# GpSimd in place of VectorE for one low part per pair in the RWKV-7 branch

## The chip, the cores and the metric

The kernel runs on one core of a Trainium2 chip. The metric is the time of the device for one launch, in microseconds (us). One execution was also taken with the hardware profiler; its trace gives start and duration of the instructions of every engine: TensorE (PE in the rows, PEld for its weight loads), VectorE (DVE), ScalarE (ACT), GpSimd (POOL) and SyncE (SP), which issues most of the loads.

## The reference, cut to what matters

A one-layer decoder trunk: RMSNorm, one combined input projection, two recurrent branches (HGRN2 and RWKV-7), a gated merge with an output projection, and a mixture of experts. The change touches the RWKV-7 branch alone and alters no value.

```python
z = xn @ w_in[l]                                  # xn: 512 x 2048
zq, zf, zi, zo, zs, zga, zgb = jnp.split(z, IN_SPLITS, axis=-1)
# RWKV-7, per head of 64 channels, one step per token:
sa = jnp.einsum('bhvk,bhk->bhv', state, at)
state = state * exp(lw) + sa * b + v * k
y = jnp.einsum('bhvk,bhk->bhv', state, rt)
# then: mean and variance over the head, rsqrt, scale, + bonus * v, * g
```

## The kernel before

The projection `xn @ w_in` is made in fp32 precision out of three fp32r products. Each weight block of 2048 x 128 (a "unit") is loaded by SyncE into a raw tile of 128 x 2048 (`in_raw`). ScalarE rounds it to a high part (`ring_hi`, L187, tile `in_hi`), and VectorE subtracts to get the low part (`ring_lo`, L192, tile `in_lo`). TensorE then runs 48 matmuls of 128x512 per unit (`dense_pass`, L160): high x high, high x low and low x high over 16 row blocks. There are two slots of each tile, so the units go round a ring. Three counters order it: `hi_done`, `lo_done` and `unit_done`. SyncE loads a unit into a slot once `lo_done` says that the unit two before has its low part, since the raw tile is free then.

The RWKV phase treats 16 heads as eight pairs, p = 0 to 7. In the first seven TensorE runs five units per pair, woven as filler (`dense(n)`) between the small matmuls of the recurrence, which works on eight chunks of 64 tokens. Each engine has one fixed list of work per pair, and a semaphore wait holds up all that stands behind it on that engine.

Where a pair ends, the lists are these.

- TensorE: six state matmuls (L1375), each behind the state that VectorE made before it, with three filler matmuls in between. Then 28 small matmuls (L1382, `y_done`), two for the bonus sum (L1386 and L1387, `bonus_sum`), 16 filler matmuls, then a wait for `sum_lo` and two matmuls for the variance (L1390 and L1391, `var_done`), and the remaining filler. The next pair begins with L1255.
- ScalarE: when unit 3 of the pair has been used (`unit_done`), it rounds the sixth unit, number 5, which is the first unit of the next pair (L187). After it come the sigmoid of a gate (L918), the squares of y (L991) and their high part (L994, `sum_hi`), and after the variance a logarithm (L996) and an exponential (L998).
- VectorE: six state updates (L1159), then the low part of unit 5 (`split(5)`, through L192), then bonus times v (L1164, waits for `bonus_sum`), the low part of the squares (L1167, waits for `sum_hi`, signals `sum_lo`), the normalisation (L1170 to L1174), and the output (L1177). The next pair begins with copies (L1046) and token shifts (L1055). Its own `split(1)` comes after L1077.
- GpSimd: stores the gate of unit 3 (L852), waits for the output, splits it into high and low (a cast at L355, a subtraction at L357), stores it (L359) and stores the other gate (L852).

The helper that moves from one engine to the other is this:

```python
def ring_lo(dve, ring, slot, m):
    dve.wait_ge(ring["hi_done"], m + 1)
    dve.tensor_tensor(ring["lo"][slot][:], ring["raw"][slot][:], ring["hi"][slot][:].bitcast(F32),
                      ALU.subtract).then_inc(ring["lo_done"], 1)
```

Of the kernel before, what the change touches and what calls it, by code (L numbers as in the profile page):

```python
# [140 lines left out]
def wait_apart(eng, passed, sem, value):  # L141


    eng.wait_ge(sem, value)
    eng.sem_inc(passed, 1)
# [44 lines left out]
# [4 lines that stand above are left out]
# [159 lines left out]
def store_split(pool, io, y, row, split, count, stored):  # L353

    pool.tensor_copy(y[:, 1, :], y[:, 0, :].bitcast(F32)).then_inc(split, 1)  # L355
    wait_apart(pool, io["pool_waits"], split, count + 1)
    pool.tensor_tensor(y[:, 0, :], y[:, 0, :].bitcast(F32), y[:, 1, :].bitcast(F32), ALU.subtract).then_inc(split, 1)  # L357
    wait_apart(pool, io["pool_waits"], split, count + 2)
    pool.dma_start(io["y_split"][bass.ds(row, 1)].rearrange("a p c t -> p (a c) t"), y[:].bitcast(F32)).then_inc(stored, 16)  # L359
# [357 lines left out]
def phase_rwkv(nc, io, keep, block, sems, early):  # L717
# [9 lines left out]
    FIRST = 3 + 3  # L727
    UNITS = 3 + HG_GATES
    LAST_UNITS = 2 * HG_GATES
    BASE = (HEADS - 1) * (4 + HG_GATES) + 4  # L730
# [6 lines left out]
    with ExitStack() as ctx:  # L737
        mem = Memory(nc, ctx)
        ring, z, z_read = keep["ring"], keep["z"], keep["z_read"]
# [66 lines left out]
        def gate_rows(p, last):  # L806

            own = [HG_GATES * (HEADS + p) + g for g in range(HG_GATES)]
            return own + [HG_GATES * (HEADS - 1) + g for g in range(HG_GATES)] if last else own

        @block.sync
        def _(sp):
            for u in range(3):
                ring_load(sp, ring, u % 2, BASE + u, w_in[:, :, (LORA_COL, LORA_COL + P, LORA_COL + 288 - P)[u]:][:, :, 0:P])

            def lora(p, col):
                wait_apart(sp, ring["passed"], lora_done, 3 * p + 3)
                up = lambda w: w[:, bass.ds(col, P)]
                sp.dma_start(w_wa[0:HALF, :], up(io["rw_w_up"][0])).then_inc(lora_in, 16)
                sp.dma_start(w_wa[HALF:P, :], up(io["rw_a_up"][0])).then_inc(lora_in, 16)  # L820
                sp.dma_start(w_g1[:], up(io["rw_g_up"][0][0:P, :])).then_inc(lora_in, 16)
                sp.dma_start(w_g2[96:P, :], up(io["rw_g_up"][0][P:, :])).then_inc(lora_in, 16)

            def pair_units(p, q, last):

                cols = [] if last else [RW_COL + WIDTH * u + P * (p + 1) for u in range(3)]
                cols += [GATE_COL + P * row for row in gate_rows(p, last)]
                for u, col in enumerate(cols):
                    ring_load(sp, ring, (q + u) % 2, BASE + FIRST + UNITS * p + u, w_in[:, :, bass.ds(col, P)])

            for u in range(3):
                ring_load(sp, ring, (3 + u) % 2, BASE + 3 + u, w_in[:, :, RW_COL + WIDTH * u:RW_COL + WIDTH * u + P])
            with sp.Fori(0, PAIRS // 2 - 1) as j:
                for q in range(2):
                    lora(2 * j + q, P * (2 * j + q))
                    pair_units(2 * j + q, q, False)
            for q in range(2):
                lora(PAIRS - 2 + q, P * (PAIRS - 2 + q))
                pair_units(PAIRS - 2 + q, q, q == 1)

        @block.gpsimd
        def _(pool):
            pool.sem_inc(y_free, 1)
            pool.sem_inc(gate_free, 1)

            def store(p, q, half, last):
                def store_gate(g):

                    u = g if last else 3 + g
                    wait_apart(pool, keep["pool_waits"], z_read[(q + u) % 2],  # L850
                               TURN + UNITS * half + (FIRST + UNITS * q + u) // 2 + 2)
                    pool.dma_start(io["gate"][bass.ds(gate_rows(p, last)[g], 1)].rearrange("a p t -> p (a t)"),  # L852
                                   gates[g][:]).then_inc(gate_stored, 16)

                for g in range(LAST_UNITS if last else 1):
                    store_gate(g)
                if last:
                    return
                wait_apart(pool, keep["pool_waits"], y_ready, p + 1)
                store_split(pool, io, y_out, HEADS + p, y_split, 2 * p, y_stored)  # L860
                store_gate(1)
                pool.wait_ge(y_stored, 16 * p + 16)
                pool.sem_inc(y_free, 1)
                pool.wait_ge(gate_stored, 16 * HG_GATES * (p + 1))
                pool.sem_inc(gate_free, 1)

            with pool.Fori(0, PAIRS // 2 - 1) as j:
                for q in range(2):
                    store(2 * j + q, q, j, False)
            for q in range(2):  # L870
                store(PAIRS - 2 + q, q, PAIRS // 2 - 1, q == 1)
# [138 lines left out]
        def _(dve):  # L1010
# [29 lines left out]
            def pair(p, q, half, last):  # L1040
                order = Order(dve, dve_o, DVE_STEPS * p)
                tt = dve.tensor_tensor
                split = lambda u: ring_lo(dve, ring, (q + u) % 2, BASE + FIRST + UNITS * p + u)
# [8 lines left out]
                for u in (1, 2):  # L1052
# [23 lines left out]
                cum_c = chunked(cum)  # L1076
                tt(chunked(dl), cum_c[:, :, RW_CHUNK - 1:RW_CHUNK].to_broadcast([P, N_CHUNKS, RW_CHUNK]), cum_c,  # L1077
                   ALU.subtract).then_inc(decays_ready, 1)
                split(1)

                dve.wait_ge(w_a_ready, 2 * p + 2)
# [74 lines left out]
                for c in range(1, N_CHUNKS - 1):  # L1156
# [1 line left out]
                    dve.wait_ge(s_ready, (N_CHUNKS - 1) * p + c)  # L1158
                    dve.scalar_tensor_tensor(state[:, c + 1, :], state[:, c, :], g_last[:, c:c + 1],  # L1159
                                             twin[1][:, 1, HALF * c:HALF * c + HALF], ALU.mult, ALU.add).then_inc(s_ready, 1)  # L1160
                split(5)

                dve.wait_ge(bonus_sum, p + 1)
                tt(bonus[:], twin[1][:, 0, :], v[:], ALU.mult).then_inc(bonus_read, 1)  # L1164
# [32 lines left out]
            with dve.Fori(0, PAIRS // 2 - 1) as j:  # L1197
                for q in range(2):
                    pair(2 * j + q, q, j, False)
            for q in range(2):  # L1200
                pair(PAIRS - 2 + q, q, PAIRS // 2 - 1, q == 1)
# [1377 lines left out]
```

## Time and profile before

| | |
|---|---|
| time, median of three runs | 2668.78 us (2668.69 to 2672.29) |
| time of the profiled execution | 2672.34 us |
| its span, first to last instruction | 2670.7 us |
| TensorE matmul busy | 2517.0 us, 94% |
| VectorE busy | 1135.8 us, 43% |
| ScalarE busy | 815.6 us, 31% |
| GpSimd busy | 105.6 us, 4% |
| RWKV phase in the trace | about 586 to 1290 us |
| seven pairs of it | one every 80.1 us |

A row of a timeline gives the start in us from the beginning of the span, the duration in us, the engine, the line of the kernel, the operation, the tiles (output, arrow, inputs), their shapes, and in brackets the idle time of the engine before the instruction, with what ended it. A matmul's end is modelled: neighbouring 128x512 matmuls start 0.23 us apart although each is shown as 0.39 us long. A busy share of 94% is therefore not TensorE at its peak, but a gap in the starts is time lost.

### The profile page before, as it was taken

What the parts mean: (1) busy time and instruction counts of PE and PEld (TensorE: products, weight loads), DVE (VectorE), ACT (ScalarE), POOL (GpSimd) and SP (SyncE); (2) the same over time, 40 slices, a digit from 0 to 9 for tenths busy, and PEclk for the clock granted to TensorE, in tenths of its full rate; (3) what the DMA queues carried; (4) which work ended last, traced back from release to release, by engine and by line L of the source; (5) the groups of instructions that cost most, each with busy time, mean ns of one, the idle gap of its engine ahead of it and who ended that gap; (6) DMA issues with size and microseconds to landing.
All of it is one profiled execution on the core that took longest, in us unless ns stands there. A gap on an engine that the chain in (4) does not pass through costs nothing.

```text
span 2670.7 us, 40372 instructions
## 1 busy us (share of the span) xinstructions
PE 2517.0 (94%) x15789; PEld 1695.0 (63%) x15789; DVE 1135.8 (43%) x1648; ACT 815.6 (31%) x1010; POOL 105.6 (4%) x136
## 2 busy tenths in 40 slices
PE   7999999999999999999999998898999989998896
PEld 5888888877787777787788876333333333333342
DVE  5333433344666666666444233332333223323234
ACT  5333444443344445444322222021111111111112
POOL 0000000010000000000000000000000000000000
PEclk9999999999999999999999999899999999999998
DMA  5333333333223232223754534999999999999995
GB/s 169 95 110 110 97 100 93 110 99 93 83 68 88 78 95 80 83 69 92 246 147 141 170 104 187 397 421 421 422 421 422 421 422 422 422 421 422 422 421 218
DMA packets 312384, 594.43 MB, mean 223 GB/s; under 512 B 17098, under 2 KB 238918, under 8 KB 260550
## 3 DMA queue, kind: packets, MB, share of 16 engines
q1 hardware_dynamic: 303372, 559.71, 57.2%
q0 software_dynamic: 8912, 33.22, 3.2%
q8 instruction: 83, 1.36, 0.2%
q14 instruction: 17, 0.14, 0.0%
HBM read 578.02 MB, written 24.64 MB: 226 GB/s over the span
## 4 chain that ended last, share of the span: by engine, by line
PE 75%; DMA 17%; DVE 3%; issue 2%; ACT 1%; SPq 0%; DVEq 0%; ACTq 0%
PE in_z L160 36%; DMA ex_w_up<-in_expert_w_up_dram 17%; PE bank L2399 10%; PE bank L2426 4%; PE bank L2386 1%; PE in_z L150 1%; PE in_z L152 1%; PE mg_z_rw L152 1%; PE mg_z_rw L150 1%; PE in_z L151 1%; PE mg_z_rw L151 1%; DVE in_lo L192 1%; PE rw_b L1315 1%; PE bank L2387 1%; PE in_z L1603 1%
## 5 line engine op out<-in xcount | busy, mean ns | idle before, releaser
L160 PE MATMUL in_z<-xn_hi,in_hi 128*128 128x512 f32 x1440 | 569.4, 395 | 4.7 <-DVE in_lo L192 3.2
L160 PE MATMUL in_z<-xn_hi,in_lo 128*128 128x512 f32 x1440 | 571.7, 397 | 0.0
L160 PE MATMUL in_z<-xn_lo,in_hi 128*128 128x512 f32 x1440 | 564.2, 392 | 0.0
L2399 PE MATMUL bank<-ex_w_gate,ex_xt_sb 128*64 128x512 f32 x768 | 359.3, 617 | 55.9 <-DMA ex_w_up<-in_expert_w_up_dram 55.9
L192 DVE TENSOR_TENSOR in_lo<-in_raw,in_hi 128x2048 fp32r<-128x2048 f32 x122 | 281.6, 2308 | 284.0 <-ACT in_hi L187 167.7
L2401 PE MATMUL bank<-ex_w_up,ex_xt_sb 128*64 128x512 f32 x768 | 360.1, 618 | 0.0
L160 PEld LDWEIGHTS in_z<-xn_hi,in_hi 128*128 128x128 f32 x1440 | 271.1, 188 | 64.9 <-issue 5.3
L160 PEld LDWEIGHTS in_z<-xn_lo,in_hi 128*128 128x128 f32 x1440 | 270.8, 188 | 58.0 <-issue 1.9
L160 PEld LDWEIGHTS in_z<-xn_hi,in_lo 128*128 128x128 f32 x1440 | 271.0, 188 | 55.5
L2399 PEld LDWEIGHTS bank<-ex_w_gate,ex_xt_sb 128*64 128x64 f32 x768 | 104.9, 142 | 278.9 <-issue 278.8
L2426 PE MATMUL bank<-ex_w_down,const 128*64 128x512 f32 x512 | 227.8, 598 | 2.4 <-ACT const L2312 0.6
L2428 PE MATMUL bank<-ex_w_down,const 128*64 128x512 f32 x512 | 227.9, 598 | 0.0
L2165 DVE TENSOR_TENSOR h<-bank,h 128x512 f32<-128x512 f32 x240 | 149.0, 682 | 178.1 <-PE bank L2387 177.9
L187 ACT ACTIVATE in_hi<-in_raw 128x2048 fp32r<-128x2048 f32 x89 | 169.7, 1907 | 46.2 <-PE in_z L160 43.1
L2155 DVE SCALAR_TENSOR_TENSOR logits_t<-bank,rs_slot,logits_t 64x512 f32<-64x512 f32 x32 | 23.8, 744 | 345.2 <-ACT logits_t L2310 344.7
L2310 ACT ACTIVATE logits_t<-bank,rs_slot 64x512 f32<-64x512 f32 x32 | 21.9, 683 | 485.2 <-PE bank L2401 485.2
L2426 PEld LDWEIGHTS bank<-ex_w_down,const 128*64 128x64 f32 x512 | 67.9, 137 | 138.5 <-issue 138.4
L2320 ACT ACTIVATE ex_y_rows<-bank,ex_w_slot 64x512 f32<-64x512 f32 x128 | 87.4, 683 | 220.2 <-PE bank L2428 217.7
L1520 ACT ACTIVATE in_hi<-in_raw 128x2048 fp32r<-128x2048 f32 x30 | 57.5, 1918 | 234.4 <-PE mg_z_rw L152 122.5
L2401 PEld LDWEIGHTS bank<-ex_w_up,ex_xt_sb 128*64 128x64 f32 x768 | 104.9, 141 | 0.0
L2386 PE MATMUL bank<-ex_y_high,const_as_r 128*128 128x512 f32 x240 | 100.8, 420 | 0.0
L2191 DVE TENSOR_TENSOR ex_y_low<-ex_y_rows,ex_y_high 128x1024 fp32r<-128x1024 f32 x32 | 39.2, 1226 | 132.4 <-ACT ex_y_high L2324 132.4
(505 smaller groups left out, 3481.9 us busy)
## 6 DMA issues: line engine op xcount, KB each, us to landing
ex_w_down<-in_expert_w_down_dram SPq DMA_DIRECT2D x128, 1024.0 KB, 21.2
ex_w_gate<-in_expert_w_gate_dram SPq DMA_DIRECT2D x96, 1024.0 KB, 23.0
ex_w_up<-in_expert_w_up_dram SPq DMA_DIRECT2D x96, 1024.0 KB, 26.0
in_raw<-in_w_in_dram SPq DMA_DIRECT2D x91, 1024.0 KB, 5.7
in_raw<-in_w_out_dram SPq DMA_DIRECT2D x32, 512.0 KB, 4.7
ex_w_gate0b<-in_expert_w_gate_dram SPq DMA_DIRECT2D x16, 1024.0 KB
ex_w_up0b<-in_expert_w_up_dram SPq DMA_DIRECT2D x16, 1024.0 KB
rt_then_ex_w<-in_expert_w_gate_dram SPq DMA_DIRECT2D x16, 1024.0 KB
```

What stands on the lines that cost most here:

```text
L150: pe.matmul(out, w_hi, x_hi, start=first, stop=False, skip_group_check=True)
L160: return pe.matmul(out, w[:, k, :], x[:, k, :], start=(n == 0), stop=(n == PASSES * KT - 1), skip_group_check=True)
L187: act.activation(ring["hi"][slot][:], ring["raw"][slot][:], ACT.Copy).then_inc(ring["hi_done"], 1)
L192: dve.tensor_tensor(ring["lo"][slot][:], ring["raw"][slot][:], ring["hi"][slot][:].bitcast(F32), ALU.subtract).then_inc(ring["lo_done"], 1)
L1520: act.activation(ring["hi"][slot][:], ring["raw"][slot][:], ACT.Copy).then_inc(ring["hi_done"], 1)
L2165: dve.tensor_tensor(part, bank[SPREAD_BANKS[o]][:], part, ALU.add).then_inc(added, 1)
L2320: act.activation(y[halves[u], f:f + D_EXPERT], down_ps[c][part, :], ACT.Copy, scale=w_slot[part, :]).then_inc(y_read, 1)
L2386: pe.matmul(bank[b][:], rows, y_hi[:, f:f + D_EXPERT], start=True, stop=False, skip_group_check=True)
L2399: pe.matmul(gate_up[low, :], x_t[:, k, halves[u]], w_gate[n][u][:, j, :], start=start, stop=stop, skip_group_check=True)
L2401: mm = pe.matmul(gate_up[high, :], x_t[:, k, halves[u]], w_up[n][u][:, j, :], start=start, stop=stop, skip_group_check=True)
L2426: pe.matmul(down_ps[c][low, :], h_t[:, n, :], w_down[n][:, lo_c:lo_c + D_EXPERT], start=(n == 0), stop=(n == DC - 1), skip_group_check=True)
L2428: mm = pe.matmul(down_ps[c][high, :], h_t[:, n, :], w_down[n][:, hi_c:hi_c + D_EXPERT], start=(n == 0), stop=(n == DC - 1), skip_group_che ...
```

## The change

For the first seven pairs GpSimd makes the low part of unit 5. It is put ahead of the gate stores in GpSimd's list of the pair. VectorE does it only in the last pair. Since `lo_done` is one counter that both engines now raise, VectorE waits, before its `split(1)`, until the low part of unit 0 of the pair (the one that GpSimd made) has been counted.

```diff
@@ GpSimd, store(p, q, half, last)
+                if not last:
+                    ring_lo(pool, ring, (q + 5) % 2, BASE + FIRST + UNITS * p + 5)
                 for g in range(LAST_UNITS if last else 1):
                     store_gate(g)
@@ VectorE, pair(p, q, half, last)
                    ALU.subtract).then_inc(decays_ready, 1)
+                dve.wait_ge(ring["lo_done"], BASE + FIRST + UNITS * p + 3)
                 split(1)
@@ VectorE, behind the state updates
-                split(5)
+                if last:
+                    split(5)
```

## Rows read from the trace of the kernel before

**Rows 1.** The page's busy time by engine, and its chain of waits by engine.

```profile
PE 2517.0 (94%) x15789; PEld 1695.0 (63%) x15789; DVE 1135.8 (43%) x1648; ACT 815.6 (31%) x1010; POOL 105.6 (4%) x136
...
PE 75%; DMA 17%; DVE 3%; issue 2%; ACT 1%; SPq 0%; DVEq 0%; ACTq 0%
```

**Rows 2.** The seven pairs' stretch: busy us (count) by engine, granted clock, DMA share.

```profile
640.00:1260.00 620.00, 615.21 (x6738) 486.96 (x6737) 401.98 (x539) 278.10 (x351) 27.39 (x37) 1.00 0.30 82
```

**Rows 3.** TensorE's waits in that phase: line <- releaser: us total, times, longest.

```profile
PE in_z L160 <- DVE in_lo L192: 3.2, 9, 1.6
```

**Rows 4.** VectorE by time, first pair: start us, us, instruction [idle before].

```profile
715.25 0.28 DVE L1159 SCALAR_TENSOR_TENSOR rw_tm<-rw_tm,rw_g_last,rw_b 128x64 f32<-128x64 f32 x1 [0.63 <-PE rw_b L1375]
716.56 2.29 DVE L192 TENSOR_TENSOR in_lo<-in_raw,in_hi 128x2048 fp32r<-128x2048 f32 x1 [1.03 <-ACT in_hi L187]
718.77 0.68 DVE L1164 TENSOR_TENSOR rw_k<-rw_b,rw_v 128x512 f32<-128x512 f32 x1
720.30 0.69 DVE L1167 TENSOR_TENSOR rw_kb_r<-rw_sq,rw_kb_r 128x512 fp32r<-128x512 f32 x1 [0.85 <-ACT rw_kb_r L994]
...
728.35 0.91 DVE L1055 TENSOR_TENSOR rw_lw<-rw_zc 128x512 f32<-128x512 f32 x1 [0.21 <-DVE rw_one_ka L1048]
729.18 1.76 DVE L1055 TENSOR_TENSOR rw_cum<-rw_zc 128x512 f32<-128x512 f32 x1
...
738.32 0.69 DVE L1074 TENSOR_SCALAR rw_sq<-rw_b 128x512 f32<-128x512 f32 x1 [2.16 <-PE rw_b L1262]
...
740.12 2.28 DVE L192 TENSOR_TENSOR in_lo<-in_raw,in_hi 128x2048 fp32r<-128x2048 f32 x1
```

**Rows 5.** ScalarE in order of time, first pair.

```profile
714.62 1.91 ACT L187 ACTIVATE in_hi<-in_raw 128x2048 fp32r<-128x2048 f32 x1 [6.15 <-PE in_z L160]
716.55 1.28 ACT L918 ACT_TABLE_LOAD   x1
...
719.57 0.63 ACT L994 ACTIVATE rw_kb_r<-rw_sq 128x512 fp32r<-128x512 f32 x1
...
721.82 0.69 ACT L996 ACTIVATE rw_ba<-rw_b,rw_eps 128x512 f32<-128x512 f32 x1 [0.32 <-PE rw_b L1391]
```

**Rows 6.** TensorE in order of time, around two hand-overs from VectorE.

```profile
720.82 0.39 PE L160 MATMUL in_z<-xn_hi,in_lo 128*128 128x512 f32 x1
721.05 0.50 PE L1390 MATMUL rw_b<-rw_kb_r,rw_block_r 128*128 128x512 f32 x1
...
741.90 0.39 PE L160 MATMUL in_z<-xn_hi,in_lo 128*128 128x512 f32 x1
742.54 0.49 PE L160 MATMUL in_z<-xn_hi,in_hi 128*128 128x512 f32 x1 [0.25 <-DVE in_lo L192]
```

**Rows 7.** GpSimd in order of time, first pair.

```profile
719.24 0.55 POOL L852 DMA_DIRECT2D scratch_gate<-rw_e_neg  x1 [128.74 <-ACT rw_e_neg L918]
728.10 0.61 POOL L355 CAST rw_y_out<-rw_y_out 128x512 fp32r<-128x512 f32 x1 [8.31 <-DVE rw_y_out L1177]
728.90 1.50 POOL L357 TENSOR_TENSOR rw_y_out<-rw_y_out 128x512 fp32r<-128x512 f32 x1 [0.18 <-POOL rw_y_out L355]
```

**Rows 8.** The one 128x2048 GpSimd subtraction, in the norm phase.

```profile
20.75 4.54 POOL L316 TENSOR_TENSOR in_lo<-in_raw,in_hi 128x2048 fp32r<-128x2048 f32 x1 [20.18 <-ACT in_hi L268]
```

**Rows 9.** ScalarE ahead of it: the rounding that releases it.

```profile
18.76 1.91 ACT L268 ACTIVATE in_hi<-in_raw 128x2048 fp32r<-128x2048 f32 x1 [2.77 <-DMA in_raw<-in_w_in_dram]
```

**Rows 10.** VectorE beside it; two inputs from PSUM and SBUF.

```profile
21.50 5.36 DVE L308 SCALAR_TENSOR_TENSOR xn_lo<-x_tr,par,xn_hi 128x512 fp32r<-128x512 f32 x8 [3.03 <-ACT xn_hi L273]
```

**Rows 11.** Instructions of one line: xcount: ns min/median/max, first and last start.

```profile
L1167 DVE TENSOR_TENSOR rw_kb_r<-rw_sq,rw_kb_r x8: 691/693/694, 720.3 to 1287.0; 128x512 fp32r<-128x512 f32 x8
...
  PEld rw_b L1390: 1.9, 7
```

**Rows 12.** A GpSimd subtraction of the HGRN2 phase.

```profile
586.21 3.11 POOL L357 TENSOR_TENSOR hg_y<-hg_y 128x512 fp32r<-128x512 f32 x1 [0.18 <-POOL hg_y L355]
```

**Rows 13.** VectorE in the same microseconds.

```profile
585.64 2.53 DVE L192 TENSOR_TENSOR in_lo<-in_raw,in_hi 128x2048 fp32r<-128x2048 f32 x1 [0.40 <-ACT in_hi L187]
```

## The prediction, made before the result was known

> **What bounds the kernel now.** I read the page first: TensorE is busy for 94% of the span and carries 75% of the chain of waits, VectorE 3% [rows 1]. In the stretch that the change touches this is sharper: of 620 us TensorE's matmuls fill 615.21, VectorE's work 401.98 and GpSimd's 27.39, at a full clock [rows 2]. So a microsecond saved on VectorE is worth something only where TensorE waits for it. Of those waits, the one on low parts comes to 3.2 us in nine times [rows 3], and the timeline shows that the regular one is not the low part being moved but `split(1)` of the next pair: it ends at 740.12 + 2.28 = 742.40, and the matmul behind it starts at 742.54, 0.64 us after its neighbour where 0.23 is usual [rows 4, 6]. The low part of unit 5 is ready at 718.85 and first used by TensorE after 730, in the next pair. Nobody waits for it.
>
> What happens behind it decides. ScalarE ends the high part of unit 5 at 714.62 + 1.91 = 716.53, loads a table, makes a gate and the squares, and ends the squares' high part (L994) at 720.20 [rows 5]. VectorE has finished the low part by then, has done L1164, and sits idle for 0.85 us until ScalarE releases L1167, which runs from 720.30 to 720.99 [rows 4]. TensorE's L1390 needs it and starts at 721.05, just 0.23 us behind its neighbour of 720.82 [rows 6]: no time is lost, but none is spare either, for its weight load was held in seven pairs, 1.9 us in all [rows 11]. The pairs repeat this within hundredths; L1167 lasts 691 to 694 ns in all eight [rows 11].
>
> **The change part by part.** *Removed from VectorE:* seven subtractions of 2.29 us, 16.0 us [rows 4]. L1164 moves up by about 1 us, to the end of the bonus matmuls, and then VectorE waits longer for ScalarE: L1167 is released by L994, whose place in ScalarE's list does not change. Gain on the path: 0. Were ScalarE earlier, L1390 still could not start before its neighbours are done.
>
> *Added to GpSimd:* seven subtractions of the same tiles. The norm phase has one: 4.54 us, starting 0.08 us after the high part that releases it (20.67 to 20.75) [rows 8, 9]. The state chain is over at 715.53 [rows 4] when the high part is still being made, so this work cannot lie beside the chain. With 0.10 us to pick it up, GpSimd runs it from 716.63 to 721.17. TensorE wants the result nine microseconds later, so its length alone costs nothing. But it covers 720.30, where VectorE starts L1167, an operation with both inputs in SBUF (`rw_sq`, `rw_kb_r`).
>
> *What the two do to each other* stands in the same trace, one pair boundary on. GpSimd's subtraction of 128x512 (L357) starts at 728.90, while VectorE is in a shift of two SBUF inputs: that shift takes 0.91 us, where L1167 of the same size takes 0.69. The next shift starts at 729.18 and takes 1.76 us, to 730.94; GpSimd's ends at 730.40 [rows 4, 7]. A quarter of 4.54 us is 1.14 us, and the second shift lost 1.07 us: it stood still for as long as GpSimd's operation ran, and ended 0.54 us after it. In the HGRN2 phase the order is the other way: VectorE's low part started first and lost only 2.53 - 2.29 = 0.24 us, while GpSimd's subtraction took 3.11 us instead of 1.14 [rows 12, 13]. The one that comes second stands still. An operation with one input in PSUM is not touched: eight of L308 beside the 4.54 us operation take 5.36 us, 0.67 each [rows 8, 10]; L1164 is of that kind.
>
> In the changed kernel GpSimd is first. L1167 stands still until about 721.17 and ends 0.54 us later, at 721.71, which is 0.72 us later than 720.99. TensorE then has run out of work: the hand-over takes 0.14 us in the second case of [rows 6], against the 0.06 us that it takes at 721.05 now. So L1390 starts at 721.71 + 0.06 to 0.14, 0.72 to 0.80 us late. I take 0.80, as the stalled hand-over is the one that resembles it. Seven pairs: 5.6 us.
>
> Rows show a hold of about 1.1 us, not one of 4.5 us. If GpSimd gave the port away in the middle, L1167 would lose less. From below: nothing, or the 0.24 us that the first comer lost [rows 13], 1.7 us over seven pairs. From above: L1164 stands still too, ends at 721.71, and L1167 follows a pitch of 0.60 us behind, a delay of 1.40 us with the hand-over, 9.8 us in all. I take the full hold of L1167 alone, since all of the 1.1 us hold in the rows was exclusive.
>
> The Trainium skill, "SBUF — State Buffer", section "Who interferes with whom", says that a VectorE instruction with two SBUF inputs and a GpSimd instruction that reads SBUF exclude each other, that the first comer keeps the shared pair for its whole instruction, and that the other blocks fully. By this rule the hold lasts the whole 4.54 us, and the sum is the 5.6 us above; the trace agrees for the 1.1 us case. Against my 4.54 us speaks "Perfetto Trace Analysis", section "GPSIMD Engine Instruction", which calls the spans of GpSimd instructions in a profile unreliable. Should the reads be over early, the sum would be smaller; the 0.54 us between the two ends, read at VectorE, is the check that this trace allows.
>
> *What the stall moves.* L1391, L996, L998 and the normalisation follow L1390, all later by the same 0.80 us as TensorE's own filler. VectorE reaches the next pair that much later, but so does TensorE, and VectorE's L1074 waits 2.16 us for TensorE there anyhow [rows 4]. So the delay neither grows nor is won back, and everything behind the phase moves with it.
>
> *Moved on GpSimd:* the gate store of 719.24 [rows 7] stands behind the subtraction and goes out at about 721.2. Its tile is written again after 741; no cost. *Moved on SyncE:* the load that `lo_done` of unit 5 releases goes out near 721.2 instead of 718.9 and is for a high part that ScalarE makes after 744; no cost, and SyncE has only loads of later units behind it. If that cover were gone, at most the 2.3 us that the low part is later would be at stake.
>
> *Added wait on VectorE:* before `split(1)`, at 740.12, for a count reached at 721.2, 19 us before. Behind it stands the low part that TensorE does wait for, so what the instruction itself takes would be lost. VectorE's sequencer runs ahead of operations of 0.6 us pitch; I take 0, at most 0.1 us each, 0.7 us in all.
>
> **The sum.** Profiled execution: 2672.34 + 5.6 = 2677.9 us. It lies 3.56 us above the median of the runs shown; the same 5.6 us on the median 2668.78 gives 2674.4 us.
>
> **The rivals.**
> - *GpSimd does not stop L1167, or lets it in early.* It decides from the point where GpSimd holds its reads for less than 720.30 - 716.63 = 3.67 us, or hands the port over between pieces. Then the change costs 0 to 1.7 us: 2668.8 to 2670.5, no change. For it: rows show only holds of 128x512. Against it: the second shift got nothing for its whole wait [rows 4, 7].
> - *The hold is wider*, L1164 included: 9.8 us, 2678.6 us. Against it: L308 ran at its pace beside GpSimd [rows 10].
> - *Faster.* VectorE is 2.29 us lighter per pair, and the regular wait before 742.54 goes away. That would give back 0.64 - 0.23 = 0.41 us in seven pairs, 2.9 us: 2665.9. Against it: VectorE waits for TensorE at L1074 in between [rows 4], so what it gains earlier does not reach `split(1)`.
> - That GpSimd's work is beside the state chain, as the change says, I hold to be wrong by 1.1 us, 715.53 against 716.63; it is part of every case.
>
> **How the numbers follow.** The forecast (5 to 7 us slower) has 0.61, the first rival 0.22, the wider hold 0.11, the faster one 0.06. A measurement of this kernel tells about 0.2%, 5.3 us, from no change, and the forecast lies almost on that line: a little over half of its chance, 0.38, is beyond it. Slower by over 0.2%: 0.38 + 0.11 = 0.49. Faster by over 0.2%: 0.03, half of that rival's chance, since its own price stays below the line. Within: 0.23 + 0.22 + 0.03 = 0.48. Though the two are as good as even, the time is that of the forecast. The range runs from just below the first rival, 2667.8, to just above the wider hold, 2679.3; the forecast's own is 2673.3 to 2676.0.
>
> **What would show it.** Right: in the seven pairs GpSimd's `in_lo` starts about 0.1 us after L187 ends and lasts 4.5 us; L1167 lasts about 1.4 us instead of 0.69 and ends some 0.54 us after it; L1390 starts 0.8 us late with idle time in front of it that names L1167; L1164 keeps 0.68 us; the pairs come every 80.9 us instead of every 80.1. Wrong: L1167 keeps 0.69 us (first rival), L1164 is stretched (wider hold), or the idle time before the matmul that follows `split(1)` shrinks (faster).

## The result, and the profile after

The changed kernel takes 2677.88 us (median of nine, 2677.43 to 2680.34), the kernel before 2672.29 us in the nine runs beside it (2668.69 to 2675.65). The ratio is 1.0024, with a 95% interval from 1.0015 to 1.0033: slower by 0.24%, which is 6.4 us (interval 4.0 to 8.8 us); between the two medians lie 5.6 us. The profiled span grew from 2670.7 to 2676.1 us.

The page's row of busy times, after, against [rows 1]:

```profile
PE 2516.7 (94%) x15789; PEld 1693.7 (63%) x15789; DVE 1125.5 (42%) x1641; ACT 815.5 (30%) x1010; POOL 137.3 (5%) x143
```

VectorE lost 10.3 us of busy time and GpSimd gained 31.7, seven operations of 4.6 us. VectorE gave up seven times 2.29 = 16.0 us, so 5.7 us came back; 7 x 0.78 = 5.5 of them are time in which it stood still, as the next rows show. VectorE in the first pair, after (start us, us, instruction, idle time before it), against [rows 4]; the lines of the kernel have moved by up to four:

```profile
715.24 0.28 DVE L1162 SCALAR_TENSOR_TENSOR rw_tm<-rw_tm,rw_g_last,rw_b 128x64 f32<-128x64 f32 x1 [0.64 <-PE rw_b L1379]
717.61 0.69 DVE L1168 TENSOR_TENSOR rw_k<-rw_b,rw_v 128x512 f32<-128x512 f32 x1 [2.09 <-PE rw_b L1391]
720.28 1.47 DVE L1171 TENSOR_TENSOR rw_kb_r<-rw_sq,rw_kb_r 128x512 fp32r<-128x512 f32 x1 [1.98 <-ACT rw_kb_r L996]
...
739.08 0.69 DVE L1076 TENSOR_SCALAR rw_sq<-rw_b 128x512 f32<-128x512 f32 x1 [2.16 <-PE rw_b L1266]
...
740.89 2.28 DVE L192 TENSOR_TENSOR in_lo<-in_raw,in_hi 128x2048 fp32r<-128x2048 f32 x1
```

ScalarE and GpSimd there, against [rows 5, 7]:

```profile
714.60 1.91 ACT L187 ACTIVATE in_hi<-in_raw 128x2048 fp32r<-128x2048 f32 x1 [6.16 <-PE in_z L160]
...
719.55 0.63 ACT L996 ACTIVATE rw_kb_r<-rw_sq 128x512 fp32r<-128x512 f32 x1
...
722.58 0.69 ACT L998 ACTIVATE rw_ba<-rw_b,rw_eps 128x512 f32<-128x512 f32 x1 [1.10 <-PE rw_b L1395]
```

```profile
716.60 4.60 POOL L192 TENSOR_TENSOR in_lo<-in_raw,in_hi 128x2048 fp32r<-128x2048 f32 x1 [126.17 <-ACT in_hi L187]
721.16 0.56 POOL L852 DMA_DIRECT2D scratch_gate<-rw_e_neg  x1
```

ScalarE ends the high part at 716.51. GpSimd starts at 716.60, 1.1 us after the last state update has ended, and works until 721.20. The bonus multiplication (now L1168, one input in PSUM) moves up to 717.61 and keeps 0.69 us. The split of the squares (now L1171, both inputs in SBUF) starts at 720.28 as before, released by ScalarE, and takes 1.47 us instead of 0.69: it ends at 721.75, 0.55 us after GpSimd.

TensorE, after, against [rows 6]; the last two rows are the end of the second pair and the start of the third, which is a turn of the loop over pairs:

```profile
720.82 0.39 PE L160 MATMUL in_z<-xn_hi,in_lo 128*128 128x512 f32 x1
721.81 0.50 PE L1394 MATMUL rw_b<-rw_kb_r,rw_block_r 128*128 128x512 f32 x1 [0.60 <-DVE rw_kb_r L1171]
...
743.30 0.49 PE L160 MATMUL in_z<-xn_hi,in_hi 128*128 128x512 f32 x1 [0.25 <-DVE in_lo L192]
...
809.10 0.39 PE L160 MATMUL in_z<-xn_hi,in_lo 128*128 128x512 f32 x1
810.68 0.66 PE L1259 MATMUL rw_b<-rw_low,rw_w_wa 64*128 64x512 f32 x1 [1.20 <-issue]
```

L1394 (before: L1390) starts 0.99 us behind its neighbour where 0.23 was enough: 0.76 us. The wait for `split(1)` is what it was, 0.25 us. Then there is something that the prediction does not have. At the turn TensorE stands for 1.20 us in front of L1259, with nothing in the profile that it waited for. The same place before:

```profile
807.57 0.39 PE L160 MATMUL in_z<-xn_hi,in_lo 128*128 128x512 f32 x1
808.08 0.66 PE L1255 MATMUL rw_b<-rw_low,rw_w_wa 64*128 64x512 f32 x1
```

TensorE's waits from 620 to 1290 us, after (total, times, longest), against [rows 3]:

```profile
PE rw_b L1394 <- DVE rw_kb_r L1171: 4.3, 7, 0.7
PE in_z L160 <- DVE in_lo L192: 3.2, 9, 1.5
...
PE rw_b L1259 <- issue: 2.3, 2, 1.2
```

So there are two new groups of idle time: seven times 0.60 us in front of the variance matmuls, and 2.3 us at the two turns of the loop (1.20 and 1.07), where before had 0 and 0.23.

The start of the first pair to the start of the eighth is the measure that the experiments below use, since it holds all that was touched: 1208.42 - 647.91 = 560.51 us before, 1215.77 - 647.87 = 567.90 us after, 7.39 us more. In the shares of the seven pairs this is 0.80, 1.84, 0.76, 1.61, 0.89, 0.76 and 0.73 us; the two large ones are the pairs that end at a turn. What follows the eighth start took 1462.3 us before and 1460.3 after, and in the other traces of this study that leave it alone from 1459.3 to 1465.0 us, without order. This scatter of the rest (its cause was not looked for) is why a difference of 2 us is seen in the stretch and not in the median.

### The profile page after: what moved, and what is told of

The parts are those of the page before. It is cut to its first block, busy times and chain, and to the rows that moved or that the text cites. A ratio compares the mean times of both kernels' runs of the same rounds, so it can differ in the third digit from the quotient of the medians.

```text
span 2676.1 us, 40374 instructions
## 1 busy us (share of the span) xinstructions
PE 2516.7 (94%) x15789; PEld 1693.7 (63%) x15789; DVE 1125.5 (42%) x1641; ACT 815.5 (30%) x1010; POOL 137.3 (5%) x143
## 4 chain that ended last, share of the span: by engine, by line
PE 74%; DMA 16%; DVE 4%; ACT 2%; issue 2%; SPq 0%; DVEq 0%; ACTq 0%
PE in_z L160 35%; DMA ex_w_up<-in_expert_w_up_dram 16%; PE bank L2403 11%; PE bank L2430 4%; PE bank L2390 1%; PE in_z L150 1%; PE in_z L151 1%; PE mg_z_rw L151 1%; PE mg_z_rw L150 1%; PE in_z L152 1%; PE mg_z_rw L152 1%; DVE in_lo L192 1%; PE rw_b L1319 1%; PE bank L2391 1%; ACT in_hi L187 1%
## 5 line engine op out<-in xcount | busy, mean ns | idle before, releaser
L192 DVE TENSOR_TENSOR in_lo<-in_raw,in_hi 128x2048 fp32r<-128x2048 f32 x115 | 265.5, 2309 | 276.7 <-ACT in_hi L187 160.4
```

## The experiments

Twelve further runs were made, eleven of them of other kernels. "Stretch" is the time from the first to the eighth pair's first matmul in each one's trace. Times are compared with the kernel before on the same chip.

| kernel | stretch, us | idle at the two turns, us | squares' split, us | ratio to before (95%) |
|---|---|---|---|---|
| before | 560.51 | 0, 0.23 | 0.69 | |
| changed | 567.90 | 1.20, 1.07 | 1.47 | 1.0024 (1.0015 to 1.0033) |
| e12_after_again (the changed kernel) | 568.03 | 1.27, 0.99 | 1.46 | one run, 2677.97 us |
| e1_wait_only | 560.86 | 0.29, 0.27 | 0.69 | 0.9999 (0.9990 to 1.0008) |
| e3_half | 561.34 | 0.29, 0.52 | 0.69 | 0.9997 (0.9988 to 1.0006) |
| e9_twelve | 562.74 | 1.03, 0.89 | 0.69 | one run, 2673.72 us |
| e10_fourteen | 563.98 | 1.09, 1.05 | 0.91 | one run, 2675.75 us |
| e2_psum_operand | 565.60 | 1.85, 1.85 | 0.69 | 1.0028 (1.0017 to 1.0038) |
| e7_memsets | 566.44 | 2.37, 2.26 | 0.69 | 1.0025 (1.0016 to 1.0034) |
| e4_behind | 566.90 | 0, 0, then 2.3 and 2.5 behind them | 0.69 | 1.0024 (1.0015 to 1.0033) |
| e5_dve_late | 562.93 | 1.24, 1.61 | 0.69 | 1.0007 (0.9998 to 1.0016) |
| e6_small_load | 566.10 | 0, 0 | 1.46 | 1.0026 (1.0017 to 1.0035) |
| e8_split1_early | 556.73 | 0.28, 0 | 0.69 | 0.9986 (0.9977 to 0.9995) |
| e11_both_early | 556.86 | 0, 0 | 0.69 | 0.9976 (0.9966 to 0.9986) |

### The wait alone

```diff
+                dve.wait_ge(ring["lo_done"], BASE + FIRST + UNITS * p + 3)
                 split(1)
```

> The kernel before with the new wait on VectorE alone; VectorE still makes the low part of unit 5. Theory (GpSimd's subtraction keeps VectorE's two-SBUF-input operation L1167 standing): the wait costs nothing, 0 to 0.7 us on the kernel before, and the matmul behind split(1) keeps its 0.17 to 0.25 us of idle time. Rival (the wait, or the count that it reads, makes the difference): 5 to 6 us slower, with the loss in front of the matmul behind split(1).

Measured: 2671.24 against 2671.01 us. TensorE's waits for the low parts are the old ones, those of [rows 3]:

```profile
PE in_z L160 <- DVE in_lo L192: 3.2, 9, 1.6
```

The new wait costs nothing that can be seen. The count that it waits for had been reached long before.

### How much of the tile GpSimd reads

The code is written shorter here than in the kernels.

```diff
-                    ring_lo(pool, ring, (q + 5) % 2, BASE + FIRST + UNITS * p + 5)
+                    pool.wait_ge(ring["hi_done"], BASE + FIRST + UNITS * p + 6)
+                    pool.tensor_tensor(lo[:, 0:K, :], raw[:, 0:K, :], hi[:, 0:K, :], ALU.subtract)   # K = 8, 12, 14 of 16
```

> The changed kernel, but GpSimd subtracts only 1024 of the 2048 columns (half of the low part of unit 5 is left out). Theory: GpSimd's operation lasts 2.3 us, from 716.6 to 718.9, is over before 720.3, so VectorE's split of the squares keeps 0.69 us, and the time is that of the kernel before, within 1 us; freeing VectorE of the work gains nothing. A rival in which GpSimd's being used at all, or the new order of the counts, costs the time expects 5 us slower still; a rival in which the lighter VectorE is worth something expects 1 to 3 us faster than before.

> The changed kernel, with GpSimd subtracting 1536 of the 2048 columns (the last quarter of the low part is left out). Theory: its operation lasts 3.45 us, 716.6 to 720.05, just short of the 720.28 at which VectorE's split of the squares starts: that keeps 0.69 us and TensorE does not wait in the pairs. The released load is 1.1 us earlier than in the changed kernel, so the idle time at the two turns lies between before's 0 to 0.3 us and the 1.85 us of the kernel with the PSUM operand. Rival (the hold goes on after the operation has ended, or depends on something else than overlap): 0.8 us or more.

> The changed kernel, with GpSimd subtracting 1792 of the 2048 columns (the last eighth is left out). Theory: its operation ends at 720.6 and VectorE's split of the squares, started at 720.28, stands still until then: it ends 0.54 us after it, at 721.2, and so lasts 0.9 us instead of 0.69 (0.69 at 1536 columns, 1.47 at 2048); TensorE's idle time in front of the variance matmul is about 0.1 us. Rival (the hold is of one length once it catches VectorE): 1.4 us or more as with 2048 columns.

Measured: with 1024 columns the time is that of before, 2671.01 us for both, and the stretch is 0.8 us longer, 0.6 of it at the two turns. VectorE's split of the squares keeps its length:

```profile
719.90 0.69 DVE L1174 TENSOR_TENSOR rw_kb_r<-rw_sq,rw_kb_r 128x512 fp32r<-128x512 f32 x1 [1.98 <-ACT rw_kb_r L999]
```

It keeps it with 1536 columns too, where GpSimd takes 3.50 us instead of the 3.45 expected and still ends short of the split. With 1792 columns GpSimd's end and the split overlap, first pair (GpSimd, then VectorE):

```profile
716.98 4.04 POOL L858 TENSOR_TENSOR in_lo<-in_raw,in_hi 128x1792 fp32r<-128x1792 f32 x1 [126.19 <-ACT in_hi L187]
```

```profile
720.66 0.91 DVE L1174 TENSOR_TENSOR rw_kb_r<-rw_sq,rw_kb_r 128x512 fp32r<-128x512 f32 x1 [1.99 <-ACT rw_kb_r L999]
```

GpSimd ends at 721.02 and the split 0.55 us later, at 721.57. TensorE's variance matmul then starts 0.44 us behind its neighbour instead of 0.23, a loss of 0.2 us where about 0.1 was expected. So the split takes 0.69, 0.69, 0.91 and 1.47 us at 1024, 1536, 1792 and 2048 columns: where the two overlap, it ends 0.55 to 0.56 us after GpSimd's operation, in all seven pairs of both kernels. The point from which the "not slower" rival decides, 3.67 us, lies between 3.50 (no hold) and 4.04 (held). The half kernel also shows that a VectorE lighter by 2.29 us in seven pairs gains nothing here. With 1536 and 1792 columns the turns cost 0.9 to 1.1 us each, which is most of what the first of these two kernels loses in the stretch and half of what the second does.

### One input from PSUM, and a GpSimd that only writes

```diff
-                tt(sum_parts[1], sq[:], sum_parts[0].bitcast(F32), ALU.subtract).then_inc(sum_lo, 1)
+                tt(sum_parts[1], twin[1][:, 0, :], sum_parts[0].bitcast(F32), ALU.max).then_inc(sum_lo, 1)
```

> The changed kernel, but VectorE's split of the squares takes its first input from PSUM (the bonus sum, of the same shape) in place of SBUF, with a maximum for the subtraction: the variance is not the reference's. Theory: an operation with one SBUF input does not meet GpSimd, so it keeps 0.69 us beside GpSimd's 4.6 us, and the seven stalls are gone: 5.3 us less than the changed kernel, less what the turns of the loop cost. On the turns: if the later load is their cause, their idle time stays and grows by up to 0.76 us each (2 to 4 us slower than before in all); if TensorE's stall is the cause, none and the time of before. Rival to the theory (any VectorE operation is held while GpSimd reads): the operation lasts 1.47 us and the time is that of the changed kernel, 5 to 6 us above before.

GpSimd and VectorE, first pair:

```profile
715.64 4.59 POOL L192 TENSOR_TENSOR in_lo<-in_raw,in_hi 128x2048 fp32r<-128x2048 f32 x1 [125.50 <-ACT in_hi L187]
```

```profile
719.33 0.69 DVE L1171 TENSOR_TENSOR rw_kb_r<-rw_b,rw_kb_r 128x512 fp32r<-128x512 f32 x1 [1.99 <-ACT rw_kb_r L996]
```

The operation lies inside GpSimd's 4.59 us and keeps 0.69: with one SBUF input it is not held. (It is also a maximum in place of a subtraction; L1168 of the changed kernel, a multiplication with one input in PSUM, is not held either.) The second kernel keeps VectorE's instruction and changes GpSimd's (shortened; `lo5` is the tile of the low part):

```diff
-                    ring_lo(pool, ring, (q + 5) % 2, BASE + FIRST + UNITS * p + 5)
+                    wait_apart(pool, keep["pool_waits"], ring["hi_done"], BASE + FIRST + UNITS * p + 6)
+                    pool.memset(lo5[:, 0:8, :], 0.0)     # and, each behind the one before it,
+                    pool.memset(lo5, 0.0)
+                    pool.memset(lo5, 0.0).then_inc(ring["lo_done"], 1)
```

> The changed kernel, but GpSimd fills the low part with zeros by three memsets (0.9 and twice 1.8 us with 0.2 us between, about 716.6 to 721.5) instead of subtracting: it is as busy across 720.3, and reads nothing from SBUF; the low part of the unit is left out. Theory (it is GpSimd's reading that VectorE's second SBUF input meets): VectorE's split of the squares keeps 0.69 us, no idle time in front of the variance matmuls; with the later load at the turns 2 to 5 us slower than before. Rival (any GpSimd operation on SBUF holds VectorE): the split of the squares lasts until the memset running at 720.3 ends, 1.2 us or more longer, in seven pairs.

```profile
717.02 1.81 POOL L862 MEMSET in_lo<- 128x2048 f32 x1 [0.15 <-POOL in_lo L860]
```

```profile
717.57 0.69 DVE L1177 TENSOR_TENSOR rw_kb_r<-rw_sq,rw_kb_r 128x512 fp32r<-128x512 f32 x1 [1.99 <-ACT rw_kb_r L1002]
```

The split starts 0.55 us into a memset of 1.81 us and ends before it, unheld. In these runs both halves of the condition are needed: two SBUF inputs on VectorE, and a GpSimd operation that reads SBUF.

Yet neither kernel was fast. Their stretches are 5.1 and 5.9 us longer than before, with idle time at the turns of 1.85 us and more. The turns can carry a loss of this size by themselves. In these two kernels and in e4_behind another 1.6 to 1.7 us are lost in the pair that follows the second turn. The trace shows where: TensorE's granted clock falls there to 0.50 for 3.41 us, the lower of its two levels (1.2 instead of 2.4 GHz), which costs half of that time. In the kernel with the PSUM operand, in the columns of [rows 2], just behind the second turn and after it:

```profile
971.70:975.10 3.40, 3.40 (x7) 1.51 (x5) 3.33 (x6) 1.20 (x2) 1.10 (x2) 0.50 0.55 220
975.20:978.60 3.40, 3.40 (x16) 2.70 (x15) 1.91 (x2) 3.02 (x4) 0.00 (x0) 1.00 0.02 6
```

Before it fell, TensorE had stood for 1.85 us up to 970.79. The same idle time at the first turn of this kernel was not followed by a fall. In the other eleven traces the clock is not lowered anywhere in the stretch.

### GpSimd behind the split of the squares

```diff
+                    pool.wait_ge(sum_lo, 3 * p + 3)
                     ring_lo(pool, ring, (q + 5) % 2, BASE + FIRST + UNITS * p + 5)
```

> The changed kernel, with GpSimd waiting for the split of the squares on VectorE (sum_lo) before its subtraction, which then runs from about 721.1 to 725.7; TensorE wants it at about 730. Theory, first part: VectorE's split of the squares keeps 0.69 us and the seven stalls of 0.76 us in front of the variance matmuls are gone. Second part (the trace of the changed kernel shows 1.20 and 1.07 us of idle time of TensorE at the two turns of the loop over pairs, where the trace of before shows 0 and 0.23; the 1 MB load that lo_done of unit 5 releases then runs 3 us closer to the turn): the load here goes out at 725.9, so it runs right across the turn, and the idle time there is 1.2 us or more, twice: 2 to 5 us slower than before in all. Rival to the second part (the idle time at the turn comes from TensorE's own stall in the pair): none at the turn, and the time is that of before, within 1 us.

Measured: 2676.6 us, 1.0024, as slow as the changed kernel, with no hold in any pair. The first part holds. The second holds in kind, with more than the 1.2 us each that it asked for, though the idle time has moved to the filler matmuls behind the turn:

```profile
PE in_z L160 <- issue: 4.8, 2, 2.5
```

The stretch is 6.4 us longer than before and the median 5.6 us higher, more than the 2 to 5 us expected. The 6.4 us are 4.8 us of this idle time, and 1.7 us of the lowered clock.

### The late low part without GpSimd

```diff
-                split(5)
-
                 dve.wait_ge(bonus_sum, p + 1)
...
                 tt(sum_parts[1], sq[:], sum_parts[0].bitcast(F32), ALU.subtract).then_inc(sum_lo, 1)
+                split(5)
```

> The kernel before, with no work moved to GpSimd: VectorE makes the low part of unit 5 behind its split of the squares instead of ahead of it (about 721.0 to 723.3). No engine shares anything new, TensorE's matmuls in front of the variance are not held, and only lo_done of unit 5 and with it the 1 MB load of the unit two behind come 4.4 us later. Theory (the load that runs into the turn of the loop over pairs holds up what TensorE needs to go on there): idle time of TensorE of 1.5 to 2.5 us at or just behind each of the two turns, 3 to 6 us slower than before, as with the two kernels in which GpSimd did the work without a stall in the pair. Rival (GpSimd's subtraction or its stores cause the idle time at the turn): none beyond the 0.2 to 0.3 us of before, and its time within 1 us.

Measured: idle times of 1.24 and 1.61 us at the turns, the stretch 2.42 us longer, in a kernel in which GpSimd does nothing new:

```profile
PE rw_b L1254 <- issue: 2.9, 2, 1.6
```

That is less than the 3 to 6 us expected, and the total (2673.14 against 2670.95, an interval that includes 1) cannot tell it from nothing. The idle time itself is clear, and GpSimd is not its cause.

### The load cut to a sixteenth

The edit is shortened here.

```diff
+                    if q == 0 and u == 2:
+                        wait_apart(sp, ring["passed"], ring["lo_done"], BASE + FIRST + UNITS * p + u + 1)
+                        sp.dma_start(ring["raw"][u % 2][:, 0:1, :], w_in[:, 0:1, bass.ds(col, P)]).then_inc(...)
+                        continue
```

> The changed kernel, but in every other pair the load that lo_done of unit 5 releases (the third of SyncE's five) brings 64 KB in place of 1 MB; the rest of that weight block keeps old values. Those are the loads ahead of the two turns of the loop. Theory: the seven stalls of L1394 stay (0.60 us of idle time each, 5.3 us in all), but the 1.20 and 1.07 us at the turns fall to 0.3 or less, so the time is 2 us below the changed kernel. Rival (the idle time at the turn is a consequence of TensorE's own stall, or of GpSimd): both stay and the time is that of the changed kernel.

All waits of TensorE in the stretch and the last pair:

```profile
PE rw_b L1398 <- DVE rw_kb_r L1175: 4.3, 7, 0.7
PE in_z L160 <- DVE in_lo L192: 3.2, 9, 1.5
PE in_z L1431 <- issue: 2.5, 1, 2.5
PE rw_b L1329 <- issue: 0.9, 1, 0.9
PE rw_b L1323 <- DVE rw_step L1134: 0.6, 1, 0.6
```

The row of the turn is gone, the seven holds of 0.60 us stand as they were, and the stretch falls by 1.80 us to 566.10. The total did not follow: 2678.59 against 2677.88 us, where 2 us less was expected. The intervals of the two ratios (1.0017 to 1.0035 and 1.0015 to 1.0033) overlap almost wholly, so the totals cannot tell 2 us; what this run shows rests on the stretch. Left over are 5.59 us more than before in the stretch, about the size of the prediction's sum; the seven holds of 0.76 us are 5.3 of them.

The two rows of SyncE show what had moved, the load that the low part of unit 5 releases in the second pair, before and after:

```profile
799.12 0.37 SPq L181 DMA_DIRECT2D in_raw<-in_w_in_dram  x1
```

```profile
802.23 0.37 SPq L181 DMA_DIRECT2D in_raw<-in_w_in_dram  x1
```

It goes out 3.1 us later, 0.76 of it TensorE's own shift, and still 7.3 us before the turn is due; before it was 9.0. By this distance, from the load's issue to the matmul's start without its idle time: 9.0, 8.8 and 8.7 us (before, e1, e3) go with 0 to 0.3 us of idle time at the first turn (0.5 at e3's second); 7.6, 7.3 and 7.3 (e9, e10, changed) with 1.0, 1.1 and 1.2; 6.5 and 6.1 (e2, e7) with 1.9 and 2.4; 4.5 (e5) with 1.2 (1.6 at the second); and at 1.8 (e4) the turn is passed and 2.3 us are lost behind it.

Distance alone gives no rule, but the DMA records of the traces do. They hold packets of 16 KB of the kind `instruction` (queue 8), and one of them starts just ahead of every turn. The profile's DMA view of 0.1 us around its start, before (804.80 to 804.90) and after (807.60 to 807.70):

```profile
q8 instruction: 1, 0.02, 85.1%
```

```profile
q8 instruction: 1, 0.02, 74.9%
```

| kernel, first turn | last filler matmul | load's packets | fetch starts | first matmul behind the turn | from fetch to it | idle, us |
|---|---|---|---|---|---|---|
| e6_small_load | 808.90 | 803.1 to 804.1 | 806.18 | 809.40 | 3.22 | 0 |
| before | 807.57 | 800.1 to 805.2 | 804.84 | 808.08 | 3.24 | 0 |
| changed | 809.10 | 803.6 to 807.6 | 807.62 | 810.68 | 3.06 | 1.20 |
| e5_dve_late | 807.73 | 804.7 to 809.9 | 806.46 | 809.36 | 2.90 | 1.24 |
| e2_psum_operand | 806.61 | 802.0 to 806.2 | 805.76 | 808.85 | 3.09 | 1.85 |
| e7_memsets | 804.80 | 800.8 to 804.6 | 804.49 | 807.56 | 3.07 | 2.37 |

In all 28 turns of the 14 traces the first matmul comes 2.8 to 3.2 us after the start of this fetch. What differs is where the fetch stands against TensorE's own work: 2.7 us ahead of the last filler matmul in e6, 1.5 us in the changed kernel, 0.3 us in e7, and the idle time is longer by nearly what the fetch is later (to within 0.3 us). In e4 the load's packets run from 806.3 to 811.8, so this fetch is in time (3.05 us ahead, no idle time), and the next one is late instead: it starts 2.92 us behind the first matmul of the turn where before it was 0.25, and the filler matmul that stood for 2.3 us follows it by 2.45. So TensorE waits for instructions, and they are fetched late when the load's packets are under way. The queue does not carry the name of an engine; that it is TensorE's follows from these intervals. By what the load holds the fetch back is not shown.

### A trace of the changed kernel once more

> The changed kernel once more, unchanged, for its trace. Theory (late load into the turn): again 1 us or more of idle time of TensorE at each of the two turns of the loop over pairs. Rival (chance of one execution): 0.3 us or less.

Measured: 1.27 and 0.99 us at the turns, and the holds in all seven pairs. Both traces have the idle time at both turns, so it is part of the change's cost and not the chance of one execution.

### Where VectorE does have a gap that helps

```diff
                    ALU.subtract).then_inc(decays_ready, 1)
-                split(1)
...
+                split(1)
                 dve.wait_ge(kk_sum, p + 1)
```

> The kernel before, with VectorE's low part of unit 1 (split(1)) moved ahead of its wait for the sum of kk, into the 2.16 us in which it waits for TensorE. Its high part is ready 6 us earlier. Theory: the matmul that follows it no longer waits (0.17 to 0.25 us of idle time, 0.41 us between starts lost in each of eight pairs), the operations behind L1074 are 0.1 us later at most: 2.5 to 3.5 us less than before, about 0.1%. Rival: the load that lo_done of unit 1 releases then runs 3 us earlier and the chain of kk starts later, and TensorE waits for the operands instead: no gain or a loss of up to 1 us.

Measured: 2667.15 us, ratio 0.9986 (0.9977 to 0.9995); the stretch is 3.78 us shorter. VectorE, first pair, and what is left of TensorE's waits for low parts, once in the last pair:

```profile
735.45 2.29 DVE L192 TENSOR_TENSOR in_lo<-in_raw,in_hi 128x2048 fp32r<-128x2048 f32 x1
737.77 0.69 DVE L1075 TENSOR_SCALAR rw_sq<-rw_b 128x512 f32<-128x512 f32 x1
```

```profile
PE in_z L160 <- DVE in_lo L192: 1.5, 1, 1.5
```

A pair takes 79.5 us where it took 80.0, a little more than the 0.41 us counted. For the last wait, rounding and low part of unit 2 in the last pair go where the other pairs have them:

```diff
                 if not last:
                     read_out(0)
-                    split(2)
+                split(2)
                 act.wait_ge(tok_done, 3 * p + 1)
...
-                if not last:
-                    split(2)
+                split(2)
                 dve.wait_ge(tok_done, 3 * p + 3)
...
-                if last:
-                    split(2)
```

> The kernel with split(1) early, and in the last pair the rounding and the low part of unit 2 put where the other pairs have them, ahead of the copies of the token-major tiles. Theory: TensorE's one wait of 1.5 to 1.6 us for a low part in the last pair is gone as well: 1.5 us less than the kernel with split(1) early, 4.5 to 5 us (0.18%) less than before. Rival: ScalarE's copies in the last pair start 1.9 us later and TensorE waits for them instead: no further gain.

Measured: 2663.62 us against 2671.04, ratio 0.9976 (0.9966 to 0.9986). No wait for a low part is left among TensorE's waits from 620 to 1290 us, of which these are all:

```profile
PE in_z L1419 <- issue: 2.4, 1, 2.4
PE rw_b L1311 <- DVE rw_step L1123: 0.6, 1, 0.6
```

The first matmul of the merge (L1419) starts 69.44 us after the start of the last pair, in the kernel with split(1) early 71.16: 1.7 us, where 1.5 was expected. This version beats both kernels, the one before by 0.24%. Its interval overlaps that of the kernel with split(1) early alone, so the last step rests on the trace.

## Why the prediction was right, and where it was not

*The total.* Right. Forecast 5.6 us slower, 2674.4 us on the median shown and 2677.9 on the profiled execution; measured 5.6 us between the medians and 6.4 us by the ratio. That the medians agree to the tenth is luck: the interval of the ratio goes from 4.0 to 8.8 us, and the stretch alone shows 7.4. The kernel before had a median of 2672.29 us over nine runs where the three shown first gave 2668.78; that is why the absolute time agrees with the upper of the two figures and lies above the forecast's own bounds, 2673.3 to 2676.0. (These bounds are 4.5 and 7.2 us above 2668.78, a little wider than the "5 to 7 us" of its words.)

*VectorE's lighter list gains nothing:* right. L1171 still starts at 720.28, and with half the columns the time is that of before.

*GpSimd's work:* 4.60 us against 4.54, picked up in 0.09 us against 0.10, and beside nothing of the state chain: right.

*The hold:* right in kind and size. L1171 ends at 721.75 where 721.71 was worked out, L1394 is 0.76 us late where 0.72 to 0.80 was, and the full hold behind a long operation, which no row of before showed, is shown by the series of columns. The Trainium skill, "SBUF — State Buffer", section "Who interferes with whom", says that a VectorE instruction with two SBUF inputs contends with a GpSimd instruction that reads SBUF, and that the first to issue keeps the shared pair for the whole instruction; the latter it says beside VectorE's two-port modes. The runs agree, and for two SBUF inputs as well: 0.69, 0.69, 0.91 and 1.47 us, and no hold with the PSUM operand or the memsets. The warning of the Trainium skill on GpSimd's spans ("Perfetto Trace Analysis", section "GPSIMD Engine Instruction") did not matter here: VectorE ended 0.55 to 0.56 us behind GpSimd's shown end in every held pair.

*The added wait:* right, nothing (2671.24 against 2671.01 us in e1).

*"The delay neither grows nor is won back":* right for `split(1)`, whose wait stayed 0.25 us.

*"Moved on SyncE: ... no cost":* this step failed. Its cover was looked for with the data's reader (ScalarE after 744, which was indeed never late), and not with what else happens while the megabyte moves. At the two turns this term, put at nothing, costs 1.20 + 1.07 - 0.23 = 2.04 us. That the load is the cause is shown from both sides, by its delay alone (e5) and by its absence (e6). In the stretch it makes 7.39 us out of seven holds of 0.76, 5.3 us. In the total it is not seen as an error: 7.4 us lies within the interval of the ratio, and in the two profiled executions what follows the stretch was 2.0 us shorter in the changed kernel. What TensorE waits for at the turn is not named among the profile's waits. It stands in front of the first instructions behind a backward branch, and the fetch ahead of them starts 1.48 us before the last filler matmul where it was 2.73 before; in all traces the matmul follows the fetch by 2.8 to 3.2 us. So it is the late arrival of its own instructions. Why a load of data makes a fetch late stays open.

*The rivals.* "GpSimd does not stop L1167" fell with the 1.47 us; the wider hold with L1168's 0.69; "faster" with the unchanged 0.25 us at `split(1)`. The gain that this rival looked for exists, but needs another edit (e8).

## What to carry to other kernels

An idle GpSimd is not free help for a busy VectorE: compare the length of its operation, to the tenth of a microsecond, with the start of the next VectorE instruction that has two SBUF inputs, and see whether TensorE stands directly behind that one. Before an operation is moved, look at whether anyone waits for its result; the low part moved here had nine microseconds to spare, while one that TensorE did wait for could be had for nothing by putting it into a gap of 2.16 us on the same engine. And where a moved operation frees a buffer, follow the load that this releases not only to its reader, but to whatever it overlaps, the fetch of instructions ahead of a loop's turn above all.

## What was not expected of the hardware

- A 1 MB load shortly ahead of a turn of TensorE's loop cost TensorE 0.9 to 2.4 us there, although none of its data was late. With 64 KB in its place the idle time is 0.
- The idle time follows the 16 KB instruction fetch that the load makes late: the first matmul behind the turn starts 2.8 to 3.2 us after this fetch in all 28 turns. The distance from the load's issue to the turn is a poor measure: at 9 us the cost was 0 to 0.5 us, at 6 to 6.5 us 1.9 to 2.4, at 4.5 us 1.2 to 1.6, and at 1.8 us a loss of 2.3 to 2.5 us came behind the turn, at the next fetch.
- GpSimd's memset of 128x2048 takes 1.81 us and did not hold VectorE's instruction with two SBUF inputs. Its subtraction of the same tile takes 4.6 us and held that instruction, which then ended 0.55 to 0.56 us after GpSimd's.
